# One pass over V in place of two: segments that alternate between the column halves, with eviction by ScalarE and an accumulator in SBUF

## What is computed

```python
a = jnp.einsum("td,thkd->thk", xb, u[eb])      # the chosen experts' rows of u
act = gb * jax.nn.gelu(a)                      # gates, 8 heads x 16 chosen experts
return jnp.einsum("thk,thkd->td", act, v[eb])  # weighted sum of their rows of v
...
x = x + gate2 * peer(h2, ...)
```

## Time and profile before

| what | value |
| --- | --- |
| median of the runs | 3388.33 us |
| the profiled execution, own time | 3392.54 us |
| its span, first to last instruction | 3390.7 us |
| mean granted TensorE clock | 0.971 of 2.4 GHz |
| PE busy in the span | 3182.5 us (94%) |
| DVE busy | 2618.8 us (77%) |
| ACT busy | 1109.7 us (33%) |
| POOL busy | 754.0 us (22%) |
| DMA traffic | 883.66 MB, mean 261 GB/s |

### The profile page before, as it was taken

The page is one execution under the profiler, slowest core; times in us unless marked ns, Lnnn a source line. Parts: engine busy times, 40 slices in busy tenths (PEclk is TensorE's granted clock), DMA queues, the critical chain, the costliest instruction groups (busy, mean ns, idle before and its releaser), DMA issues.

```text
span 3390.7 us, 45823 instructions
## 1 busy us (share of the span) xinstructions
PE 3182.5 (94%) x17301; PEld 2923.6 (86%) x17301; DVE 2618.8 (77%) x3067; ACT 1109.7 (33%) x1032; POOL 754.0 (22%) x444
## 2 busy tenths in 40 slices
PE   4898967879899999999999999999999998999999
PEld 3686744457678999999999999999999998999999
DVE  6996968856763688888778888866777776777777
ACT  3323233431122444444323333332333332333332
POOL 4500000000020012222102322313333332333333
PEclk8899989979999999999999999999999999999999
DMA  8621213247744357777648888888999998999997
GB/s 348 252 92 69 81 56 130 111 162 299 269 161 165 134 197 278 277 277 277 228 169 327 340 343 334 344 305 318 349 343 348 347 347 324 349 347 348 348 347 283
DMA packets 241097, 883.66 MB, mean 261 GB/s; under 512 B 17680, under 2 KB 132496, under 8 KB 169744
## 3 DMA queue, kind: packets, MB, share of 16 engines
q1 hardware_dynamic: 161552, 545.82, 43.1%
q0 software_dynamic: 55296, 268.46, 21.2%
q10 hardware_dynamic: 24192, 68.64, 5.3%
HBM read 824.13 MB, written 58.72 MB: 260 GB/s over the span
## 4 chain that ended last, share of the span: by engine, by line
PE 78%; DVE 14%; DMA 3%; ACT 2%; issue 2%; POOL 0%; DVEq 0%; SPq 0%; ACTq 0%; PEldq 0%
PE bank L1362 12%; PE bank L1363 12%; PE bank L1364 12%; PE bank L1687 10%; PE bank L1688 10%; PE bank L1689 10%; PE bank L1662 2%; DVE w_lo L783 2%; DVE ada_w L808 2%; PE bank L1573 2%; PE bank L1574 2%; PE bank L1575 2%; DVE qk_rstd L976 1%; DMA ada_w<-wada 1%; DVE ada_w L792 1%
## 5 line engine op out<-in xcount | busy, mean ns | idle before, releaser
L783 DVE TENSOR_TENSOR w_lo<-w_raw,w_hi 128x2048 fp32r<-128x2048 f32 (+1 forms) x319 | 727.2, 2280 | 590.8 <-ACT w_hi L427 579.0
L427 ACT ACTIVATE w_hi<-w_raw 128x2048 fp32r<-128x2048 f32 (+1 forms) x327 | 621.6, 1901 | 1336.5 <-PE bank L1364 626.4
L1362 PE MATMUL bank<-act_hi,w_hi 128*128 128x384 f32 (+1 forms) x2584 | 908.0, 351 | 45.8 <-DVE w_lo L783 27.8
L1363 PE MATMUL bank<-act_lo,w_hi 128*128 128x384 f32 (+1 forms) x2584 | 900.0, 348 | 0.0
L1364 PE MATMUL bank<-act_hi,w_lo 128*128 128x384 f32 (+1 forms) x2584 | 899.9, 348 | 0.0
L1687 PE MATMUL bank<-wt_hi,w_hi 128*128 128x384 f32 x2048 | 687.9, 336 | 17.5 <-DVEq L1323 8.4
L1688 PE MATMUL bank<-wt_lo,w_hi 128*128 128x384 f32 x2048 | 685.8, 335 | 0.0
L1689 PE MATMUL bank<-wt_hi,w_lo 128*128 128x384 f32 x2048 | 685.8, 335 | 0.0
L417 POOL DMA_INDIRECT v_row<-v,vrow_i x256 | 401.3, 1568 | 734.9 <-DVE y_g L1308 655.1
L1362 PEld LDWEIGHTS bank<-act_hi,w_hi 128*128 128x128 f32 x2584 | 490.2, 190 | 78.2 <-issue 24.9
L1364 PEld LDWEIGHTS bank<-act_hi,w_lo 128*128 128x128 f32 x2584 | 489.7, 190 | 22.2
(11 more groups left out here) (244 smaller groups left out, 3128.6 us busy)
## 6 DMA issues: line engine op xcount, KB each, us to landing
w_raw<-u SPq DMA_DIRECT2D x128, 1024.0 KB, 8.1
w_raw<-v SPq DMA_DIRECT2D x128, 1024.0 KB, 5.3
ada_w<-wada SPq DMA_DIRECT2D x80, 1024.0 KB, 5.1
gelu_l<-gelu_scratch SPq DMA_DIRECT2D x64, 768.0 KB, 6.5
gate_l<-gate_scratch SPq DMA_DIRECT2D x64, 768.0 KB, 9.5
w_raw<-win SPq DMA_DIRECT2D x27, 1024.0 KB, 4.7
gelu_scratch<-gelu_s ACTq DMA_DIRECT2D x128, 192.0 KB, 5.6
gate_scratch<-g_chunk ACTq DMA_DIRECT2D x8, 3072.0 KB, 13.4
```

Source lines behind the costliest of these rows:

```text
L427: act.activation(w_hi[n0 % 2][:, 0:width], w_raw[n0 % 2][:, 0:width], ACT.Copy).then_inc(hi_done, 1)
L783: dve.tensor_tensor(w_lo[s][:, 0:width], w_raw[s][:, 0:width], w_hi[s][:, 0:width].bitcast(F32), ALU.subtract).then_inc(lo_done, 1)
L1362: pe.matmul(out, wh, hi_t(k), start=(k == 0), stop=False)
L1363: pe.matmul(out, wh, lo_t(k), start=False, stop=False)
```

## The change

The two passes become one. The 128 jobs are cut into 17 segments of 4, 14 times 8, 8 and 4 jobs. A segment works on one column half; the halves alternate as A B B A A B B, seen in groups of four jobs, so that eight groups of experts (two units) are used for both halves while their weights are in SBUF. Each of the 32 units is made once. Four buffers of wt_hi and wt_lo take the place of two; one buffer wt, multiplied in place, takes the place of wt and gelu_l.

At the end of each of the first 15 segments PE waits for its own last matmul in each bank (`seg_sum`), ACT copies each bank, scaled by the gate2 column, to an SBUF stage (`evict`), and DVE adds the stage to acc_o, which holds x1 at the start (`add`). PE's first matmul in each bank of the next segment waits for that bank's eviction. The last segment of each half closes as before: transposes of y_g, DVE's multiply and add, ACT's stores. For the half that closes first this is job 123.

The rows of v are gathered whole, 128x2048, 128 times, with the row numbers of u and into the buffers u_row; they start when the last dot is done. `v_step` handles 2048 columns, 18 in 16 jobs. The helpers that computed row numbers for half rows go. x1 (4 MB) is loaded once. PE's V stage is written as four jobs, a loop of 7 turns with 16 jobs in its body, and 12 jobs.

```diff
+def v_index(q):
+    group, pos, j = q // 8, q // 4 % 2, q % 4
+    return 64 * (pos ^ (group % 2)) + 4 * group + j
...
-        v_row = [at(f"v_row{s}", 4 * s, [P, 1024]) for s in range(4)]
+        wt_hi = [at(f"wt_hi{s}", 112 + 6 * s, [P, 4, TD], F32R) for s in range(4)]
+        wt = at("wt", 176, [P, 4, TD])
+        acc_o = at("acc_o", 0, [P, KD, T])
+        stage = [at(f"stage{d}", 32 + 1.5 * d, [P, TD]) for d in range(8)]
...
 # SP
+            def load_unit(n, turn=0):
+                if n:
+                    sp.wait_ge(wtl_ready, n + turn * 4)
+                rows = bass.ds(turn * 16 + 4 * n, 4)
+                sp.dma_start(wt[:], gelu_d[rows].rearrange("e p t -> p e t")).then_inc(wt_loaded, 16)
+                sp.dma_start(gate_l[:], gate_d[:, :, rows, :].rearrange("c p i t -> p c i t")).then_inc(wt_loaded, 16)
...
+            load_unit(0)
+            load_v(0)
+            load_unit(1)
+            load_v(1)
             for s in range(2):
                 sp.wait_ge(gelu_stored[s], DMA_LEAD + 16 * NKEY // 2)
+            load_v(2)
+            load_v(3)
+            load_unit(2)
...
+            with sp.Fori(0, 7) as i:
+                for r in range(16):
+                    load_v(8 + r, i)
+                    if r % 4 == 2:
+                        load_unit(4 + r // 4, i)
...
 # POOL
-            pool.wait_ge(pe_jobs, J_V)
             pool.wait_ge(dots_done, P)
+            for n in range(P):
+                if n >= 3:
+                    pool.wait_ge(y_g_steps, n - 1)
+                pool.indirect_dma_start(u_row[n % 3][:], None, vrow_d, ...)
...
 # ACT
+            def evict(k, half_i, turn=0):
+                for d in range(8):
+                    act.wait_ge(seg_sum, 8 * k + d + 1 + turn * 16)
+                    if k:
+                        act.wait_ge(added, 8 * (k - 1) + d + 1 + turn * 16)
+                    m = 5 * KD + 8 * half_i + d
+                    act.activation(stage[d][:], bank[d][:, 0:TD], ACT.Copy, scale=mod[:, m:m + 1]).then_inc(evicted, 1)
+            for q in range(2, 6):
+                if q == 5:
+                    evict(0, 0)
+                hi(J_V + q)
+                if q == 4:
+                    weigh_hi(2)
+            with act.Fori(0, 7) as i:
+                for r in range(16):
+                    if r % 8 == 7:
+                        evict(1 + r // 8, 1 - r // 8, i)
+                    hi(J_V + 6 + r, i * 8)
+                    if r % 4 == 0:
+                        weigh_hi(3 + r // 4, i)
...
 # DVE
+            def add(k, half_i, ds_, turn=0):
+                for d in ds_:
+                    dve.wait_ge(evicted, 8 * k + d + 1 + turn * 16)
+                    o = acc_o[:, 8 * half_i + d, 0:TD]
+                    dve.tensor_tensor(o, o, stage[d][:], ALU.add).then_inc(added, 1)
+            with dve.Fori(0, 7) as i:
+                for r in range(16):
+                    lo(J_V + 6 + r, i * 8)
+                    if r % 4 == 0:
+                        weigh(3 + r // 4, i)
+                    v_step(2 + r + (r > 3) + (r > 11), i)
+                    if r % 4 == 1:
+                        weigh_lo(3 + r // 4, i)
+                    if r in (3, 11):
+                        v_step(3 + r + (r > 3), i)
+                    if r % 8 < 2:
+                        add(r // 8, r // 8, range(4 * (r % 8), 4 * (r % 8) + 4), i)
...
 # PE, in v_job
+                    for d in range(8):
+                        opens = begin is not None and e == 0
+                        if opens and begin:
+                            pe.wait_ge(begin[0], begin[1] + d)
...
+                elif end:
+                    pe.wait_ge(seg_sum, 8 * end + turn * 16)
+                    pe.sem_inc(pe_jobs, 1)
...
+            for q in range(4):
+                v_job(q, q // 2, begin=() if q == 0 else None, end=1 if q == 3 else 0)
+            with pe.Fori(0, 7) as i:
+                for r in range(16):
+                    unit = (0, 0, 1, 1, 2, 2, 3, 3, 2, 2, 3, 3, 4, 4, 5, 5)[r]
+                    v_job(4 + r, unit, i, begin=(evicted, 8 * (r // 8) + 1 + i * 16) if r % 8 == 0 else None,
+                          end=2 + r // 8 if r % 8 == 7 else 0)
+            for e in range(12):
+                unit = (28, 28, 29, 29, 30, 30, 31, 31, 30, 30, 31, 31)[e]
+                v_job(116 + e, unit, begin=(evicted, 8 * 14 + 1) if e == 0 else (y_ready, 1) if e == 8 else None,
+                      end=1 if e in (7, 11) else 0, y_cols=1024 if e == 7 else 0 if e == 11 else None)
```

More of the change, by code:

```diff
@@ L736, in _, with weigh_hi @@
                 gelu_pair(i)
+            for s in range(2):
+                act.wait_ge(g_stored[s], DMA_LEAD + 16 * 4)
+            def weigh_hi(n, turn=0):
+                act.wait_ge(wt_ready, n + 1 + turn * 4)
+                act.activation(wt_hi[n % 4][:], wt[:], ACT.Copy).then_inc(wth_ready, 1)
             act.wait_ge(dots_done, P)
@@ L754, in _ @@
[L754 to L768, removed]
+            weigh_hi(0)
@@ L1291, in _ @@
                     dot(n + 3)
+                if n == 126:
+                    weigh(0)
+            weigh_lo(0)
+            lo(J_V)
+            weigh(1)
+            lo(J_V + 1)
+            weigh_lo(1)
             dve.wait_ge(act_g_ready, 1)
             T_.step(dve.tensor_tensor(gate_g[:], gate_g[:], a_g[:], ALU.mult))
[L1294 to L1299, removed]
@@ L1311, in prepare, with v_step @@
[L1311 to L1326, removed]
+            def v_step(m, turn=0):
+                dve.wait_ge(v_row_loaded[m % 3], 16 * (m // 3 + 1) + turn * 96)
+                dve.wait_ge(y_g_steps, m + 1 + turn * 18)
+                dve.scalar_tensor_tensor(out=y_g[:], in0=u_row[m % 3][:], scalar=gate_g[:, bass.ds(turn * 18 + m, 1)], in1=y_g[:],
+                                         op0=ALU.mult, op1=ALU.add).then_inc(y_g_steps, 1)
@@ L1351, in _ @@
-            finish(1)
+            for q in range(2, 6):
+                lo(J_V + q)
+                if q == 2:
+                    v_step(0)
+                if q == 3:
+                    v_step(1)
+                if q == 4:
+                    weigh(2)
+                if q == 5:
+                    weigh_lo(2)
+            dve.wait_ge(x1_loaded, 16)
+            with dve.Fori(0, 7) as i:
[10 more added lines that the diff above has]
+                        add(r // 8, r // 8, range(4 * (r % 8), 4 * (r % 8) + 4), i)
@@ L1353, in _ @@
+            dve.wait_ge(y_g_steps, P + 1)
+            dve.sem_inc(y_g_ready, 1)
+            for e in range(10):
+                if e == 7:
+                    close_half(1, 0, 14)
+                lo(J_V + 118 + e)
+                if e == 0:
+                    weigh(31)
+                if e == 1:
+                    weigh_lo(31)
+                if e < 2:
+                    add(14, 0, range(4 * e, 4 * e + 4))
+            close_half(0, 1, 15)
         @block.tensor
@@ L1671, in _, with v_job @@
                 pe.wait_ge(g_copied[s], LEAD + 48)
[L1673 to L1677 removed]
+            def v_job(q, unit, turn=0, begin=None, end=False, y_cols=None):
+                s = (J_V + q) % 2
+                wait_lo(pe, J_V + q, turn * 8)
+                pe.wait_ge(wtl_ready, unit + 1 + turn * 4)
+                if y_cols is not None:
+                    pe.wait_ge(y_g_ready, 1)
@@ L1692, in v_job @@
-                if stop:
-                    pe.wait_ge(y_sum, 8 * (q_pass + 1))
+                        last = pe.matmul(o, w_lo[s][:, col], th, start=False, stop=bool(end) and e == 1)
+                        if e == 1 and y_cols is not None:
+                            last = pe.transpose(bank[d][:, TD:T], y_g[:, y_cols + d * P:y_cols + (d + 1) * P], ident[:])
+                            last.then_inc(y_sum, 1)
+                        elif e == 1 and end:
+                            last.then_inc(seg_sum, 1)
```

167 lines of the change are left out of this document (51 added, 116 removed).

## The result

The change made the kernel slower by 2.3%: 3473.31 us against 3396.1 (medians of 6 runs each), ratio 1.0232, 95% interval [1.0214, 1.025]. The forecast was 3385.3, the range 3376 to 3406.

The account below looks back on a forecast made before the run. TensorE (PE) was taken to bound the kernel nearly everywhere, transfers being close to full but not waited for. Gains of 16.5 us at the pass change less 13.5 for 16 switches gave -3.0 us: 3385.3 us, range 3376 to 3406.

Parts of the forecast that it names:

- rival C: PE's V loop body no longer stays resident; six backward jumps fetch at 2.0 to 3.5 us each; 3397 to 3406; chance 0.24.
- -16.5 + 13.5: V stage: 16.5 us gained at the pass change, 13.5 us added by 16 switches; net -3.0 us.
- packets in every turn and six idle times over 2 us: Sign in the changed trace for rival C: instruction packets in every 133 us turn, and six such idle times.
- forecast A: The even trade in the V stage: 3385.3 us, own range 3378 to 3394; chance 0.50.
- PE's work and its pace: PE in V: still 128 jobs of 48 matmuls and 16 transposes; nothing of the 1065 us moves.
- What goes: Pass change in V: the 8.6 us wait for the rows' sum, and 4.1 + 1.5 for late weights, go; gain 16.5 us.
- A switch: PE waiting for its last matmul between segments: 0.54 us straight, 0.7 in the loop, 1.1 where it turns; 13.5 in all.
- Evictions and VectorE: ACT's bank reads (0.47 us each) and VectorE's work (101 of 133 us per 16 jobs) in V: cost nothing.
- DMA: V loop: traffic per job falls from 2.75 to 2.375 MB, 346 to about 299 GB/s; worth nothing in the loop.
- Entry: Start of V: the third tile's lateness stays even, taken as 0; bounds 4.1 us gained to 5 us lost.
- a hole away from a switch: Sign that the prediction is wrong: PE idle in the V loop at a place other than a switch.
- Sum: V stage: -16.5 + 13.5 = -3.0 us, taking the median from 3388.33 to 3385.3.

Follow-up runs that it names:

- a_shift1: The changed kernel with the last turn of PE's first U loop written out behind it, moving the V loop: 3395.62 us, ratio 1.0002 to the kernel before.
- b12: The kernel before with 12 jobs in the body of PE's V loop, 4 turns and 8 jobs straight: 3396.33 us (one run).
- a_unroll: The changed kernel with PE's V stage written out straight, 128 jobs and no loop: 3394.97 us, ratio 0.9994 to the kernel before.
- c1: a_unroll, and PE no longer waits for itself at the 15 switches with eviction: 3384.2 us, ratio 0.9975 to the kernel before.
- n_shift4: a_shift4 with the V loop kept and PE no longer waiting for itself at the switches, as in c1: 3444.59 us (one run).
- a_shift4: The changed kernel with four turns of PE's first U loop written out behind it, moving the V loop: 3478.47 us, ratio 1.0264 to the kernel before.

## Why the prediction was wrong, point by point

**The step that failed is that the fetching of instructions stands at nothing in the sum, and the price and the chance that rival C was given.** In -16.5 + 13.5 no term stands for the six jumps; they cost 73 us. The mechanism was named: "PE's loop body no longer stays resident", with packets in every turn and six idle times over 2 us as its marks. It was given 0.24 and 12 to 21 us; it is what happened, and it cost 73 of the 76 us between this V stage and a_shift1's (1167.5 and 1091.3). The price was built on one landing of 2.0 us, since no row showed a jump that fetches. What it misses:
- The branch alone took 6.46 us, not one landing more than 0.21. The first hole was 7.4 us against 1.2 in a_shift1.
- A second stop follows, 4.1 us long, after only four matmuls. The loop's head lies 26 instructions before a block's end, and the queue's second packet after the branch began at 2784.29, inside this stop; that PE stood for the next block is read from that.
- After that, about 1.8 us at the low clock. A turn took 146.96 us (mean of five, 2480.18 to 3214.96) against 135.02 in a_shift1: 11.9 a jump, 6.2 + 3.9 + 1.8.
- Six jumps make 73 us, as the last one cost 13.3; the other 3 are the entry, where this execution stood 4.7 us instead of a_shift1's 2.9 and then ran 3.4 us at a granted clock of 0.50.

**The chance of C.** The argument against it was that no loop showed a refetch. But the largest body in the trace had some 390 instructions, so the rows said nothing about 1600. The Trainium skill, "Runtime: NRT & Kernel Launch", Instruction fetch mechanics, gives PE 2048 instructions in blocks of 256, which makes eight blocks. I took the number as a limit on the size of the body. The runs do not bear that reading out: 1570 and 1589 instructions stayed when they touched seven blocks and were fetched anew when they touched eight, so the limit counts blocks and is one short of eight. Its other rule, that a taken branch outside a window of two pages forces a fetch, does not hold for PE here: b12's 1178 instructions on six blocks stayed.

**The parts of forecast A held for the change without the jumps**, and a_shift1 is that kernel, unaltered in V. Its -3 us as a whole cannot be told from nothing (a_shift1 1.0002, a_unroll 0.9994):
- PE's work and its pace: right. 16 x 8.32 us, as before.
- What goes: right. No wait for the rows' sum, no stop after pass 0.
- A switch. Predicted 0.54 us straight, 0.7 in the loop, 1.1 where it turns. Measured from start to start 0.64, 0.82 and 1.20 (less 0.17 for a normal step and plus 0.08 to 0.1 for a slow first one: 0.55, 0.75, 1.1). The two in the loop, in a_shift1; the releaser that the profile names is the last eviction, but c1 shows that it was PE's own wait:

```profile
2674.92 0.44 PE L1718 MATMUL bank<-wt_hi,w_hi 128*128 128x384 f32 x1 [0.48 <-ACT stage L764]
...
2742.62 0.43 PE L1718 MATMUL bank<-wt_hi,w_hi 128*128 128x384 f32 x1 [0.86 <-ACT stage L764]
```

- Evictions and VectorE at nothing: right, shown by c1. An eviction was longer than taken (0.58 against PE's 0.52 a bank), and the 4.2 us in hand covered it.
- DMA: 293 GB/s in a_shift1, 299 predicted.
- Entry: even within 2 us; PE stood 2.6 to 4.7 us for the third tile in the profiles. What the prediction did not have is a hole in the first turn, PE from 2402.14 to 2404.60 in the changed kernel, in every version of it (2.5 to 3.4 us). By the prediction's own words, a hole away from a switch speaks against it. VectorE was held by late gates:

```profile
2397.12 1.76 DVE L1298 TENSOR_TENSOR wt<-wt,gate_l 128x1536 f32<-128x1536 f32 x1 [7.00 <-DMA gate_l<-gate_scratch]
```

I did not try why they are late there and not later; x1's 4 MB and the gathers that catch up run in that time.
- Sum: -3.0 predicted for the V stage, -0.5 measured in a_shift1; the hole of the first turn, 2.6 us over a step there, is the largest term between them. How close this is owes something to luck: in V that execution had no low clock at all, while a_unroll's had three stretches of 3.4 us at a granted clock of 0.50, each of which costs about 1.5.

**Open:** why the branch takes 6.5 us when a packet's own transfer takes about 1. At the jump of the changed kernel shown above, the branch started at 2774.92, the packet ran from 2778.78 to 2779.81, and the branch ended at 2781.32, so 3.9 us pass before the packet and 1.5 after it. Open too is why eight blocks are one too many (whether PE always fetches one block ahead, for one).

## What to carry to other kernels

Before merging loops or lengthening a body, count the instructions, weight loads too (98 for 48 matmuls here), and see on how many blocks of 256 they lie; here up to seven stayed on PE, and the eighth cost 7 to 14 us at every jump. If a time changes by per cents for code written ahead of a loop, look at the instruction packets and at the duration of the loop's branch. And where no row shows a mechanism that would be paid at each turn, its price is open upwards: one landing is the lower end, not the middle.

## What the runs showed of the hardware that was not expected

- PE ran straight code of 128 jobs, some 12,500 instructions, at full pace (a_unroll), so writing this loop out cost nothing in time.
- A body that overflows by one block is not fetched for that block alone: all of it came anew, nine packets a turn.
- A wait of an engine for its own last instruction at a loop's end raised the price of a refetching jump from 10.8 to 13.6 us: a turn of 143.9 us in n_shift4 less 133.1 for 16 jobs, and one of 148.6 in a_shift4 less a_shift1's 135.0, which has the same waits.
